# Banded attention in a transformer stack: pairs of heads, fused mask and maximum, unnormalised probabilities, values summed by token

## The reference

```
q = rope(hx @ Wq) / 8        k = rope(hx @ Wk)     v  = hx @ Wv
                             kz = hz @ Wk          vz = hz @ Wv
s = [ q k^T where |i - j| <= 128, else -1e30 ;  q kz^T ;  sink of the head ]
p = softmax(s)               o = p[window] v + p[context] vz
yx = o @ Wo
```

## Time and profile before

| | |
|---|---|
| time, three runs | 3087.32 us median (3086.01 to 3090.15) |
| the profiled execution | 3090.11 us, its span 3088.3 us |
| TensorE matmul busy | 2896.0 us (94%) |
| VectorE busy | 1910.9 us (62%) |
| ScalarE busy | 1506.8 us (49%) |
| granted TensorE clock, mean | 0.962 of full |
| attention, first mask to last `ut` | 1511.91 to 1619.69 us |

### The profile page before, as it was taken

The page is one execution under the profiler, slowest core; times in us unless marked ns, Lnnn a source line. Parts: engine busy times, 40 slices in busy tenths (PEclk is TensorE's granted clock), DMA queues, the critical chain, the costliest instruction groups (busy, mean ns, idle before and its releaser), DMA issues.

```text
span 3088.3 us, 59780 instructions
## 1 busy us (share of the span) xinstructions
PE 2896.0 (94%) x23682; PEld 2727.8 (88%) x23682; DVE 1910.9 (62%) x2539; ACT 1506.8 (49%) x2021; POOL 773.5 (25%) x721
## 2 busy tenths in 40 slices
PE   6999999999999999999788999998689999985999
PEld 5999999999999999999547998997389999973899
DVE  4646647776475564764575546657856566578664
ACT  3434434444344443544355646647256465572663
POOL 1313302223042240330012312308013123160230
PEclk9999999999999999999899999999699999986999
DMA  8775666656666566665003554553035555530454
GB/s 299 246 271 200 220 217 233 204 205 232 232 204 233 203 228 211 225 236 197 25 1 122 184 192 135 195 185 129 14 116 184 192 169 192 185 104 14 138 185 154
DMA packets 152571, 548.95 MB, mean 178 GB/s; under 512 B 16784, under 2 KB 20672, under 8 KB 152000
## 3 DMA queue, kind: packets, MB, share of 16 engines
q1 hardware_dynamic: 148496, 537.99, 51.4%
q10 hardware_dynamic: 3888, 8.30, 0.7%
HBM read 544.38 MB, written 1.84 MB: 177 GB/s over the span
## 4 chain that ended last, share of the span: by engine, by line
PE 86%; DVE 7%; issue 3%; ACT 2%; ACTq 1%; POOL 1%; DMA 0%; SPq 0%; DVEq 0%; POOLq 0%
PE ps L400 26%; PE ps L402 26%; PE ps L401 25%; PE ps L427 2%; PE ps L784 1%; PE ps L763 1%; PE ps L693 1%; ACT sq L1048 1%; ACT w_hi L372 1%; PE ps L863 1%; DVE w_lo L380 0%; DMA modraw<-wmod 0%; DVE AT L1905 0%; PE ps L772 0%; POOL sq L2060 0%
## 5 line engine op out<-in xcount | busy, mean ns | idle before, releaser
L380 DVE TENSOR_TENSOR w_lo<-raw,w_hi 128x1024 fp32r<-128x1024 f32 x880 | 1143.6, 1315 | 719.4 <-ACT w_hi L372 717.5
L400 PE MATMUL ps<-h_hi,w_hi 128*128 128x256 f32 x4976 | 1418.2, 285 | 28.7 <-DVE w_lo L380 11.6
L402 PE MATMUL ps<-h_hi,w_lo 128*128 128x256 f32 x4976 | 1407.9, 283 | 0.0
L401 PE MATMUL ps<-h_lo,w_hi 128*128 128x256 f32 x4976 | 1403.5, 282 | 0.0
L372 ACT ACTIVATE w_hi<-raw 128x1024 fp32r<-128x1024 f32 x880 | 905.2, 1054 | 498.3 <-PE ps L402 496.8
L400 PEld LDWEIGHTS ps<-h_hi,w_hi 128*128 128x128 f32 x4976 | 939.7, 189 | 43.7 <-issue 28.4
L402 PEld LDWEIGHTS ps<-h_hi,w_lo 128*128 128x128 f32 x4976 | 959.6, 193 | 0.0
L401 PEld LDWEIGHTS ps<-h_lo,w_hi 128*128 128x128 f32 x4976 | 941.6, 189 | 1.5 <-issue 0.5
L2064 POOL CAST u_hi<-ut 128x256 fp32r<-128x256 f32 (+1 forms) x258 | 239.8, 929 | 1495.9 <-DVE ut L1611 788.1
L400 PE MATMUL ps<-u_hi,w_hi 128*128 128x256 f32 (+1 forms) x2064 | 589.3, 286 | 0.0
L401 PE MATMUL ps<-u_lo,w_hi 128*128 128x256 f32 (+1 forms) x2064 | 581.3, 282 | 0.0
(11 more groups left out here) (292 smaller groups left out, 1995.0 us busy)
## 6 DMA issues: line engine op xcount, KB each, us to landing
raw<-wst SPq DMA_DIRECT2D x880, 512.0 KB, 3.5
modraw<-wmod SPq DMA_DIRECT2D x132, 512.0 KB, 5.4
headraw<-wmod SPq DMA_DIRECT2D x12, 512.0 KB, 10.1
mtab<-mixtabs ACTq DMA_DIRECT2D x2, 1280.0 KB, 6.2
xT<-xin ACTq DMA_DIRECT2D x2, 1024.0 KB, 23.4
atab<-attabs ACTq DMA_DIRECT2D x1, 1024.0 KB, 6.1
out<-xT SPq DMA_DIRECT2D x1, 1024.0 KB, 4.8
skew<-sqb ACTq DMA_DIRECT2D x1, 768.0 KB, 3.3
```

The source lines that it names most:

```text
L380: dve.tensor_tensor(w_lo[:, s, :], raw[:, s, :], w_hi[:, s, :], ALU.subtract).then_inc(S("lo_ready"), 1)
L400: pe.matmul(psum, wh, hi, start=start, stop=False)
L401: pe.matmul(psum, wh, lo, start=False, stop=False)
L402: return pe.matmul(psum, wl, hi, start=False, stop=stop)
```

## The change

- The rotation and a new `nsink` (minus the 16 sinks, one VectorE operation) come before `lo_upto` on VectorE, so `lo_upto(d + 14)` moves from the end of `first_qkv_dve` to behind the rotation in `attn_dve`. A dummy exponential is issued on ScalarE before the context evacuations.
- The work goes by 16 pairs p = 2 * chunk + block: both heads of a chunk for one block of queries. The two score products of a pair stand side by side on TensorE, on rows 0 to 63 and 64 to 127, into two banks.
- The mask and the maximum are one VectorE instruction, `tensor_tensor_reduce`: out = -(scores + mask), and the minimum of that row and of minus the sink. ScalarE takes exp(-out + min).
- The probabilities are turned as they are. The copies from the transposes go half to ScalarE (L1258's place) and half to VectorE.
- The sinks of a chunk are four columns: one subtraction on VectorE, one exponential on ScalarE; the division is two operations on four columns for a chunk.
- `values`: `PTw` (128 keys by 128 queries) is now stationary and `VV` (64 columns) moves; the result is token-major. `scale` multiplies it by 1/sum on VectorE, two transposes (`turn_back`) make it channel-major again, and `head_out` copies it.
- `sw`, `pw`, `PTw` have four buffers.

```diff
 first_qkv_act, before n in range(8, 12):
+                act.activation(spare[:, 0:1], epsc[:, 0:1], ACT.Exp)
 first_qkv_dve, at its end:
-                lo_upto(dve, d + 14)
 attn_pe:
                 def scores(p):
+                    cc, qb = p // 2, p % 2
+                    if p >= 2:
+                        pe.wait_ge(S("w_sb"), 2 * (p - 1))
+                    elif p == 1:
+                        pe.wait_ge(S("w_vv"), 2)
+                    for hf in range(2):
+                        r = slice(64 * hf, 64 * hf + 64)
+                        mm = pe.matmul(ps[:, 2 - 2 * qb + hf, 0:512], AQ[r, cc, P * qb:P * (qb + 1)], AK[r, cc // 4, :],
+                                       start=True, stop=True)
+                    mm.then_inc(S("w_s"), 1)
                 def turn(p):
+                    for hf in range(2):
+                        pe.wait_ge(S("w_e"), 2 * p + p // 2 + hf + 1)
+                        if p >= 1:
+                            pe.wait_ge(S("w_pt_dve" if hf else "w_pt_act"), p)
+                        for t in range(4):
+                            mm = pe.transpose(ps[:, 4 + hf, P * t:P * (t + 1)], pw[:, 2 * (p % 2) + hf, P * t:P * (t + 1)],
+                                              ident)
+                        mm.then_inc(S("w_tr"), 1)
                 def values(p):
...
+                        for t in range(4):
+                            mm = pe.matmul(ps[:, 6 + cc % 2, o0:o0 + 64], PTw[:, 2 * qb + hf, t, :], VV[:, t, v0:v0 + 64],
+                                           start=(t == 0), stop=(t == 3))
                     mm.then_inc(S("w_pv"), 1)
+                def turn_back(cc):
+                    pe.wait_ge(S("w_on"), cc + 1)
+                    for qb in range(2):
+                        mm = pe.transpose(ps[:, 6 + cc % 2, T + P * qb:T + P * (qb + 1)], on[:, cc % 2, P * qb:P * (qb + 1)],
+                                          ident)
+                    mm.then_inc(S("w_turned"), 1)
                 scores(0)
                 scores(1)
+                for p in range(PAIRS + 2):
+                    if p < PAIRS:
+                        turn(p)
+                    if p + 2 < PAIRS:
+                        scores(p + 2)
+                    if 1 <= p <= PAIRS:
+                        values(p - 1)
+                    if p >= 3 and p % 2:
+                        turn_back((p - 3) // 2)
 attn_act:
+                for p in range(PAIRS):
+                    exponentials(p, 0)
+                    if p >= 1:
+                        turned(p - 1)
+                    exponentials(p, 1)
+                    if p % 2:
+                        act.wait_ge(S("w_sk"), p // 2 + 1)
+                        act.activation(sink_w[:, p // 2, :], sink_w[:, p // 2, :], ACT.Exp).then_inc(S("w_e"), 1)
+                turned(PAIRS - 1)
 attn_dve, behind the rotation:
+                dve.tensor_scalar(nsink[:, :], vec[:, VEC["sink"]:VEC["sink"] + 2 * DC], -1.0, None,
+                                  ALU.mult).then_inc(S("w_own"), 1)
+                lo_upto(dve, c["unit"] + 2)
+                def top(p):
+                    cc, qb = p // 2, p % 2
+                    dve.wait_ge(S("w_s"), p + 1)
+                    for hf in range(2):
+                        if p >= 2:
+                            dve.wait_ge(S("w_e"), 2 * (p - 2) + (p - 2) // 2 + hf + 1)
+                        dve.tensor_tensor_reduce(sw[:, 2 * qb + hf, :], ps[:, 2 - 2 * qb + hf, :], bandW[:, qb, :], -1.0,
+                                                 nsink[:, 2 * cc + hf:2 * cc + hf + 1], ALU.add, ALU.min,
+                                                 top_w[:, cc, 2 * qb + hf:2 * qb + hf + 1]).then_inc(S("w_sb"), 1)
...
                 top(0)
+                for p in range(PAIRS + 3):
+                    if p + 1 < PAIRS:
+                        top(p + 1)
+                        if p % 2 == 0:
+                            sinks(p // 2)
+                    if p >= 3 and p % 2:
+                        scale((p - 3) // 2)
+                    if 1 <= p <= PAIRS:
+                        turned(p - 1)
+                    if 2 <= p <= PAIRS and p % 2 == 0:
+                        divide((p - 2) // 2)
+                    if p >= 4 and p % 2 == 0:
+                        head_out((p - 4) // 2)
```

More of the change, by code:

```diff
@@ L48 @@
 PER_CHUNK = 3
-SCORE_BANK = (0, 1, 6, 7)
+PAIRS = 16
 LEVELS = 6
@@ L753, in attn_pe @@
                         mm = pe.transpose(ps[:, (7, 1)[n], P * t:P * (t + 1)], AV[:, n, P * t:P * (t + 1)], ident)
-                mm.then_inc(S("w_vt"), 1)
+                mm.then_inc(S("w_turned"), 1)
                 pe.wait_ge(S("w_rope"), 5)
[L756 to L779, removed]
+                def scores(p):
+                    cc, qb = p // 2, p % 2
[8 more added lines that the diff above has]
+                    mm.then_inc(S("w_s"), 1)
@@ L780, in values @@
+                def values(p):
+                    cc, qb = p // 2, p % 2
+                    if p == 0:
+                        pe.wait_ge(S("w_vv"), 2)
+                    if qb == 0 and cc >= 2:
                         pe.wait_ge(S("gated"), c["hid"] + cc - 1)
-                    r = slice(64 * hf, 64 * hf + 64)
-                    for t in range(4):
+                    for hf in range(2):
+                        pe.wait_ge(S("w_pt_dve" if hf else "w_pt_act"), p + 1)
                         v0 = P * (cc // 4) + 64 * hf
-                        mm = pe.matmul(ps[r, 4 + cc % 2, 0:T], VV[:, t, v0:v0 + 64], PTw[:, hf, t, :],
-                                       start=(t == 0), stop=(t == 3))
+                        o0 = P * qb + 64 * hf
+                        for t in range(4):
+                            mm = pe.matmul(ps[:, 6 + cc % 2, o0:o0 + 64], PTw[:, 2 * qb + hf, t, :], VV[:, t, v0:v0 + 64],
+                                           start=(t == 0), stop=(t == 3))
@@ L1261, in attn_act @@
[L1261 to L1272, removed]
@@ L1273, in attn_act, with exponentials @@
-                pt(31)
+                def exponentials(p, hf):
+                    act.wait_ge(S("w_sb"), 2 * p + hf + 1)
+                    if p >= 2:
+                        act.wait_ge(S("w_tr"), 2 * (p - 2) + hf + 1)
+                    n = 2 * (p % 2) + hf
+                    at = 2 * (p % 2) + hf
+                    act.activation(pw[:, n, :], sw[:, n, :], ACT.Exp, scale=-1.0, bias=top_w[:, p // 2, at:at + 1],
+                                   accum_out=sum_w[:, p // 2, at:at + 1]).then_inc(S("w_e"), 1)
@@ L1737, in head_out @@
                 def head_out(cc):
-                    dve.wait_ge(S("w_pv"), 2 * cc + 2)
+                    dve.wait_ge(S("w_turned"), cc + 3)
                     dve.wait_ge(S("ulo_ready"), hid + cc + 1)
-                    dve.tensor_copy(ut[:, cc % 2, 0:T], ps[:, 4 + cc % 2, 0:T]).then_inc(S("gated"), 1)
+                    dve.tensor_copy(ut[:, cc % 2, 0:T], ps[:, 6 + cc % 2, T:2 * T]).then_inc(S("gated"), 1)
                 top(0)
-                for n in range(32):
-                    if n + 1 < 32:
-                        top(n + 1)
-                    norm(n)
-                    if n % 4 == 2 and n > 4:
-                        head_out(n // 4 - 1)
```

93 lines of the change are left out of this document (49 added, 44 removed).

## The result

In the first comparison the changed kernel took 3048.17 us by median (3042.50 to 3052.81, four runs) and the kernel before 3086.66 (3084.45 to 3090.15, four runs): 0.9871 of its time, with a 95% interval from 0.9859 to 0.9883. The profiled execution took 3042.50 us, its span is 3040.7. It is faster, by 1.3%, and the forecast of 3045 lies 3 us under the median.

A forecast was written before the change was run, and what follows sets the result against it. A chain through TensorE and VectorE, near TensorE's own work, bounds the attention loop. An 11.9 us earlier start and chunks of 9.5 against 12.24 bring the last `ut` to 1577.0, gaining 42.7 us: 3045 us, range 3037 to 3061.

The forecast's parts named there:

- The start: Ahead of the loop, with the rotation before `lo_upto`: first mask at 1500.05 in place of 1511.91, 11.9 us earlier.
- What is late next: Ahead of the loop: `lo_upto` itself, still ending at 1500.1, with the first mask queued behind it on VectorE.
- The fused instruction: Mask and maximum on VectorE: taken at 0.75 us, between bounds of 0.69 and 1.37.
- The rival that prices it as two passes: Fused instruction on VectorE costs 1.37: chunk 10.7, 9.6 us more, 3055 us; chance 0.08.
- only from 2.4 would the change lose: Fused instruction's time: it begins to count from some 0.95, and the change loses only from 2.4.
- TensorE's terms: TensorE's work a chunk: turns 2.36, scores 2.10, values 3.96, `turn_back` 0.37, sum 8.79 us.
- The rule weighed in the prediction: Attention loop: transposes do not bring TensorE to full clock, so the stage could stay at 1.2 GHz, 3100 us.
- The rival of half the clock at first: Loop's beginning at half the clock until 1527: 11.3 us lost, 3056 us; chance 0.14.
- 16 x 0.85: Rival that score pairs on TensorE do not overlap: 13.7 us at most, 3058 us; chance 0.05.
- the signs: What would show the forecast in the trace, among them 0.6 idle before every odd pair's second turn.
- a pair of 7.4 us: Attention loop: point from which half the clock all the way decides, 3100 us and slower; chance 0.05.
- hardly a gain in itself: Values on TensorE by token: 3.96 us a chunk, where the old ones were 1.87 for half of that.

The follow-up runs named there:

- rotation_only: The kernel before with one line moved, so VectorE makes the rotation ahead of the low parts (`lo_upto`): 3074.60 us, ratio 0.9967 to the kernel before.
- late_rotation: The changed kernel with the low parts (`lo_upto`) moved back ahead of the rotation on VectorE: 3053.49 us, ratio 0.9889 to the kernel before.
- unfused: The changed kernel with mask, maximum and negation as three VectorE instructions again: 3079.93 us, ratio 0.9969 to the kernel before.
- after_again: The changed kernel run once more, unchanged, on the chip of the next three: 3040.91 us, ratio 0.9844 to the kernel before.
- same_rows: The changed kernel with both score products of a pair on rows 0 to 63, result not right: 3062.05 us, ratio 0.9909 to the kernel before.
- channel_values: The changed kernel with VectorE's copy before the fused pair, `VV` stationary, heads alternating, scaling and turn back left out: 3017.54 us, ratio 0.9771 to the kernel before.
- norm_ahead: Values by channel as well, but complete: VectorE divides before the turn, ScalarE copies all turns, scores three pairs ahead: 3020.11 us, ratio 0.9780 to the kernel before.
- run 44: Not a run's label: words of "can run 44 us at half the clock", a duration told of `same_rows`.

## Why the prediction was right

The steps by the trace, in the prediction's terms:

| step | predicted | measured |
|---|---|---|
| permutation's end to first fused | 15.02 (1500.05 - 1485.03) | 14.99 |
| first fused to first turn | 1.65 | 1.66 |
| fused instruction | 0.75 | 0.748, 0.67 start to start |
| four turns | 2.36 | 2.16 |
| two score pairs | 2.10 | 2.11 |
| values of two pairs | 3.96 | 3.68 |
| turn_back | 0.37 | 0.23 |
| idle before the odd pair's second turn | 0.7, VectorE's copy | 0.82, VectorE's copy |
| chunk | 9.5 | 8.99 |
| permutation's end to last `ut` | 92.0 | 88.8 |

- **The start** came out within 0.03 us, and `rotation_only` and `late_rotation` show it as an effect of its own. What is late next was named rightly: the split's low parts, behind a split that ScalarE makes when the last context unit is evacuated.
- **The fused instruction** lay near its lower bound, as taken. The rival that prices it as two passes put the slowdown at 9.6 us. Here `unfused` shows that the rival was mis-sized: with the masks and maxima apart the stage is 34.8 us longer. At least 17.7 of that are waits, as a row takes 1.58 and not 1.37, and the rest, at most 17.1, are the 34.1 us at half the clock, which the rival didn't have. The threshold named there, "only from 2.4 would the change lose", looks too high: at 1.58 a row the whole kernel is only 0.3% under the one before, and that with the earlier start, worth 11.5 us.
- **TensorE's terms** were a little large but for the scores. In the values I gave every group a gap (4 x 0.11); here a pair's two groups run on without any, and sixteen start 0.115 apart: 1.83 to 1.84 a pair. Eight turned in one group take 0.99 where two groups of four were put at 0.59 each. The four terms are 8.18 in place of 8.79; with 0.12 more of idle time a chunk is 0.5 shorter, eight are 4.1, and the ends gave 0.9 of it back. The gain by the trace was thus 45.9 and not 42.7.
- **The clock** was 1.00 throughout the attention in the profile of the changed kernel and in that of `after_again`. The rule weighed in the prediction (the Trainium skill, TensorE: Matmul & The Clock Gate, Part 4: PE-mode transpose) would have kept the loop at 1.2 GHz. The trace disagrees for this mixture: 2.39 of 9.0 us are transposes, and 1.00 was granted from 1500 to 1560; `late_rotation`, which starts at 0.51, is back at 1.00 from 1511. The rival of half the clock at first was nevertheless real as a mechanism: `late_rotation` shows it for 13.7 us, of which 3.6 in the loop, `rotation_only` for 10.2 and `same_rows` for 44. In the changed kernel the 11.90 idle us of the earlier trace rows are gone, and its longest wait there is 1.64; that fits the argument that scores and turns fill the stretch, but doesn't show it, since `same_rows` fell behind a wait as short. It did not come true in either of the two traces of this kernel.
- **The median** hides that the forecast's 3045 is between two series, 3048.17 and 3040.91. It is right to within what two series of this kernel differ by, no better, and that it came within 3 us of the first is in part luck: its path was 3.2 us too long, and the first series' median lies 5.7 over the execution whose trace gives the 45.9.
- **Small slips of the working** change nothing: 16 x 0.85 is 13.6 and not 13.7; the signs have 0.6 of idle time where the sum has 0.7; and a pair of 7.4 us, between 4.75 at full and 8.2 at half the clock, is some 0.85 of the time at half the clock, and not nine tenths.

What the prediction did not ask is whether the new order of values is worth its detour. It noted "hardly a gain in itself" and went on. `channel_values` shows that the other order, with the heads side by side, is 0.9 us a pair cheaper, and `norm_ahead` that the normalisation it needs fits beside it. No run takes away the copies shared by two engines, the sinks by chunk or the four buffers alone, so their parts of the 34.0 us are not known.

## What to carry to other kernels

Where a loop is a chain through engines, price each wait by what is queued ahead of the instruction that ends it: here one copy behind a scaling that waited for TensorE cost 0.82 us a chunk of 8.99, and moving two lines gave back more than its wait. Two products over 64 rows each took 1.13 us side by side and 1.98 on the same rows, and two heads' values with 64 stationary columns each took 1.09 side by side and 2.00 by token; try such a pairing before changing the layout for the sake of another engine. And an instruction's price in such a loop is not its duration: taking the fusion away added 2 x 2 x 0.9 us of VectorE to a chunk, and the chunk grew by 3.9 to 6.2, by waits and time at half the clock together.

## What the hardware showed that was not expected

- Two 64-column stationary operands whose results lie on partitions 0 to 63 and 64 to 127, instructions alternating: 16 with 128 moving columns in 1.09 us, 0.064 apart. In the kernel before, eight with 64 stationary and 256 moving columns, not alternating, took 1.87, or 0.117 for 128 columns, which points to the alternation as what halves the time. Sixteen with 128 columns stationary and 64 moving: 2.00 us, with weight loads of 1.86 us beside them.
- The weight loads probably bound these last: sixteen with 64 moving columns start 0.115 apart, and eight turns, with the same 128 stationary and 128 moving columns, 0.124 apart, so that half the moving columns save hardly anything. The mean duration of a load doesn't settle it, as 128 columns take 192 ns in the values and 144 in the turns of the same kernel.
- The fused instruction is followed by a read of its accumulator of 0.08 us, which overlaps: the next one starts 0.67 behind the one before.
- VectorE multiplies 512 columns from SBUF to SBUF in 0.486 us (median of 32, two in a row 0.88), where the copy of 512 from PSUM takes 0.685. That agrees with the Trainium skill, VectorE: DVE Perf Modes, Why PSUM operands drop a tier: a PSUM operand costs a float32 instruction of one source its double rate. While GpSimd splits `ut`, the same two multiplications take 1.36 in place of 0.88, and GpSimd's own subtraction 0.84 in place of the 0.73 of the changed kernel:

```profile
1521.02 0.88 DVE L1760 TENSOR_SCALAR pw<-pw,sum_w 128x512 f32<-128x512 f32 x2
...
1530.35 1.36 DVE L1760 TENSOR_SCALAR pw<-pw,sum_w 128x512 f32<-128x512 f32 x2
1530.58 0.84 POOL L2095 TENSOR_TENSOR h_lo<-ut,h_hi 128x256 fp32r<-128x256 f32 x1
```

- One kernel's loop can run 44 us at half the clock in one execution (`same_rows`) while its other runs are 7 to 14 us shorter. It fell behind a wait of 1.63 us that ended at 1503.01; the changed kernel has a wait of 1.64 us at the same turn (1503.51, by L1764) and was granted 1.00 all along. What decides it stays open.
